# Attention turns of a two-layer encoder: minima and exponentials first, copies of turned probabilities last

## What is computed

```python
for l in range(DEPTH):                                   # 2 layers
    h = rms_norm(x, ln_g[l])
    proj = einsum('bsd,de->bse', h, w_in[l])             # q, k, v and gate columns of mixers A, B, C
    ya = window_sink_attention(...)                      # A: 12 heads, window of +-128 keys, sink, bias
    yb = global_axial_attention(...)                     # B: 12 heads, all keys of the sequence
    yc = dilated_mixture_attention(...)                  # C: 3 groups x 8 heads, merged by their denominators
    mix = concat(ya * silu(ga), yb * silu(gb), yc * silu(gc))
    x = x + einsum('bse,ed->bsd', mix, w_out[l])
```

## Time and profile before

| what | value |
|---|---|
| median of 3 runs | 2811.5 us (2803.23 to 2812.4) |
| time of the profiled execution | 2800.2 us |
| its span, first to last instruction | 2798.1 us |
| TensorE (PE) busy | 2763.8 us, 99% of the span |
| VectorE (DVE) busy | 1630.2 us, 58% |
| ScalarE (ACT) busy | 1226.2 us, 44% |
| GpSimd (POOL) busy | 932.6 us, 33% |
| DMA | 444.25 MB, mean 159 GB/s |
| granted TensorE clock | 1.000 of full speed |

### The profile page before, as it was taken

How to read it: one execution, slowest core, us unless ns; L and a number is a source line. 1 busy time by engine, 2 the same in 40 slices (tenths; PEclk the granted TensorE clock), 3 DMA queues, 4 the chain that set the end, 5 groups by cost and what they waited for, 6 DMA issues and landing times.

```text
span 2798.1 us, 44194 instructions
## 1 busy us (share of the span) xinstructions
PE 2763.8 (99%) x14913; PEld 2482.9 (89%) x14913; DVE 1630.2 (58%) x3973; ACT 1226.2 (44%) x3017; POOL 932.6 (33%) x860
## 2 busy tenths in 40 slices
PE   8999999999999999999999999999999999999999
PEld 7888899989999999988888888999899999998887
DVE  3446644434776677667743465444357766776776
ACT  4322222226665566544542222222266654664443
POOL 0333433310574377500003334333106733774000
PEclk9999999999999999999999999999999999999999
DMA  5366666569544432464624565666694444325645
GB/s 181 111 186 187 188 185 186 171 180 248 133 128 113 133 102 82 148 238 128 200 86 140 175 196 169 199 175 190 177 250 124 109 127 129 100 69 195 208 123 180
DMA packets 420602, 444.25 MB, mean 159 GB/s; under 512 B 62519, under 2 KB 314583, under 8 KB 420380
## 3 DMA queue, kind: packets, MB, share of 16 engines
q1 hardware_dynamic: 420380, 441.44, 53.4%
HBM read 315.54 MB, written 125.80 MB: 158 GB/s over the span
## 4 chain that ended last, share of the span: by engine, by line
PE 89%; DVE 3%; issue 2%; ACT 2%; POOL 2%; DMA 1%; SPq 0%; DVEq 0%; ACTq 0%; POOLq 0%
PE bank L1444 14%; PE bank L1442 14%; PE bank L1443 14%; PE bank L1498 5%; PE bank L1500 5%; PE bank L1499 5%; PE bank L1475 5%; PE bank L1477 5%; PE bank L1476 5%; PE bank L1541 4%; PE bank L1568 2%; PE bank L1527 2%; PE bank L1528 2%; PE bank L1583 2%; PE bank L1584 2%
## 5 line engine op out<-in xcount | busy, mean ns | idle before, releaser
L1916 DVE TENSOR_TENSOR w_lo<-w_raw,w_hi 128x512 fp32r<-128x512 f32 x640 | 458.3, 717 | 455.1 <-ACT w_hi L1652 451.0
L1652 ACT CAST w_hi<-w_raw 128x512 fp32r<-128x512 f32 x640 | 395.6, 619 | 686.7 <-PE bank L1444 417.5
L1442 PE MATMUL bank<-w_hi,act_hi 128*128 128x512 f32 x1728 | 688.9, 399 | 0.0
L1444 PE MATMUL bank<-w_hi,act_lo 128*128 128x512 f32 x1728 | 678.8, 393 | 0.0
L1443 PE MATMUL bank<-w_lo,act_hi 128*128 128x512 f32 x1728 | 677.3, 392 | 0.0
L2324 POOL TENSOR_SCALAR prob<-prob,denom 128x256 f32<-128x256 f32 (+2 forms) x288 | 345.9, 1205 | 270.0 <-DVE denom L2047 269.3
L1444 PEld LDWEIGHTS bank<-w_hi,act_lo 128*128 128x128 f32 x1728 | 372.4, 216 | 53.9
L1442 PEld LDWEIGHTS bank<-w_hi,act_hi 128*128 128x128 f32 x1728 | 373.2, 216 | 50.1
L1443 PEld LDWEIGHTS bank<-w_lo,act_hi 128*128 128x128 f32 x1728 | 373.1, 216 | 48.7
L1498 PE MATMUL bank<-act_hi,w_hi 128*128 128x384 f32 x1024 | 346.7, 339 | 0.0
L1500 PE MATMUL bank<-act_hi,w_lo 128*128 128x384 f32 x1024 | 344.9, 337 | 0.0
(11 more groups left out here) (121 smaller groups left out, 4636.6 us busy)
## 6 DMA issues: line engine op xcount, KB each, us to landing
w_raw<-w_in SPq DMA_DIRECT2D x144, 512.0 KB, 4.5
w_sums<-sum_out SPq DMA_DIRECT2D x32, 1280.0 KB, 6.7
w_raw<-w_sums SPq DMA_DIRECT2D x80, 512.0 KB, 4.1
sum_in<-w_out SPq DMA_DIRECT2D x64, 512.0 KB, 5.7
heads_t<-turned SPq DMA_DIRECT2D x240, 128.0 KB, 2.4
q_t<-heads_t SPq DMA_DIRECT2D x192, 128.0 KB, 2.1
k_t<-keys_t SPq DMA_DIRECT2D x48, 384.0 KB, 5.8
w_raw<-w_out SPq DMA_DIRECT2D x32, 512.0 KB, 3.7
```

What stands on the lines that cost most here:

```text
L1442: pe.matmul(acc[t][:], hi, w_hi[:, n % W_RING, :], start=(k == 0), stop=False)
L1444: last = pe.matmul(acc[t][:], lo, w_hi[:, n % W_RING, :], start=False, stop=(k == KC - 1))
L1652: nc.scalar.copy(w_hi[:, n % W_RING, :], w_raw[:, load % W_RAW, j, :]).then_inc(w_hi_done, 1)
L1916: nc.vector.tensor_tensor(w_lo[:, n % W_RING, :], w_raw[:, load % W_RAW, j, :], w_hi[:, n % W_RING, :].bitcast(F32), ALU.subtract).then_in ...
```

## The change

The order inside a turn of the attention is another on VectorE and on ScalarE; no instruction is added or removed, and TensorE, GpSimd and SyncE keep theirs. On VectorE `invert` and `find_minima` stand first, then `take_part`, the splits of the weights, the splits of the values, the merge, `add_folded` and `scale_gate`, and `pt_copy` last (ahead only of `a_lo_part`, in two turns). On ScalarE `keep`, `fold_pair` and the splits stand first, then `exp_step`, and `pt_copy` behind it. The splits of turn 0 are written ahead of the loop, where they stood first anyway.

```diff
--- before.py
+++ after.py
@@ -1853,19 +1853,22 @@
                             head_hi(l, s, t)
 
                 heads_in_dram(act, l)
+                for c in SPLIT_AT[0]:
+                    split_hi(l, CHUNKS_IN + c)
                 for i in range(N_LOOP):
-                    for c in SPLIT_AT.get(i, ()):
-                        split_hi(l, CHUNKS_IN + c)
+                    if ends_merge(i - KEEP_LAG):
+                        keep(l, STEPS[i - KEEP_LAG]["item"])
+                    if ends_pair(i - FOLD_LAG):
+                        fold_pair(l, i - FOLD_LAG)
+                    if i > 0:
+                        for c in SPLIT_AT.get(i, ()):
+                            split_hi(l, CHUNKS_IN + c)
                     if i in VALUES_AT:
                         values_hi(l, VALUES_AT[i])
-                    if ends_pair(i - FOLD_LAG):
-                        fold_pair(l, i - FOLD_LAG)
-                    if ends_merge(i - KEEP_LAG):
-                        keep(l, STEPS[i - KEEP_LAG]["item"])
+                    if i < N_STEPS:
+                        exp_step(l, i)
                     if 0 <= i - T_LAG < N_STEPS:
                         pt_copy(l, i - T_LAG)
-                    if i < N_STEPS:
-                        exp_step(l, i)
                     for mc, _ in merge_turns(i, EXP_TURN):
                         merge_exp(l, mc)
                     for n, h in TANH_AT.get(i, ()):
@@ -2221,19 +2224,20 @@
                             head_lo(l, s, t)
 
                 heads_in_dram(dve, l)
+                for c in SPLIT_AT[0]:
+                    split_lo(l, CHUNKS_IN + c)
                 for i in range(N_LOOP):
-                    for c in SPLIT_AT.get(i, ()):
-                        split_lo(l, CHUNKS_IN + c)
-                    if ends_quad(i - MIX_LAG):
-                        take_part(l, STEPS[i - MIX_LAG]["item"])
-                    if i in VALUES_AT:
-                        values_lo(l, VALUES_AT[i])
                     if 0 <= i - NORM_LAG < N_STEPS and features_first(STEPS[i - NORM_LAG]):
                         invert(l, i - NORM_LAG)
                     if i < N_STEPS:
                         find_minima(l, i)
-                    if 0 <= i - T_LAG < N_STEPS:
-                        pt_copy(l, i - T_LAG)
+                    if ends_quad(i - MIX_LAG):
+                        take_part(l, STEPS[i - MIX_LAG]["item"])
+                    if i > 0:
+                        for c in SPLIT_AT.get(i, ()):
+                            split_lo(l, CHUNKS_IN + c)
+                    if i in VALUES_AT:
+                        values_lo(l, VALUES_AT[i])
                     for mc, _ in merge_turns(i, MIN_TURN):
                         merge_minima(l, mc)
                     for mc, _ in merge_turns(i, WEIGHT_TURN):
@@ -2246,6 +2250,8 @@
                         add_folded(l, i - FOLD_LAG)
                     for n, h in GATE_DRAIN_AT.get(i, ()):
                         scale_gate(l, n, h)
+                    if 0 <= i - T_LAG < N_STEPS:
+                        pt_copy(l, i - T_LAG)
                     if i in EARLY_SPLIT:
                         a_lo_part(l, EARLY_SPLIT[i])
```

## The result

The changed kernel took 2817.3 us in the median of 17 runs (2808.67 to 2825.85), the kernel before 2802.1 us (2799.73 to 2812.4). The ratio is 1.0047 with a 95% interval of 1.0037 to 1.0056, about +13 us. In the profiled execution the span went from 2798.1 to 2815.7 us.

What follows compares the result with a forecast made beforehand. TensorE, busy 99% of the span, was taken as the bound. Q's loss of 11.2 us less gains of 7 (A and C) and 3 (B) gave +1.2 us, put on the 2811.5 us median as 2812.5 us; range 2799 to 2828.

Steps and rivals of the forecast that it cites:

- the likeliest case: Whole kernel: time within 0.3% of before, chance 0.48, with the forecast at 2812.5 us.
- Q, 11.2 us in both layers: Section Q (turns 0 to 23): ScalarE's later copies delay TensorE's value products, 5.6 us lost a layer.
- turn 5: Section Q: the copy behind step 4's exponentials ends later, so the value product starts 1.5 us later.
- turn 17: Section Q: turn 16's minimum waits 2.92 us for a store, so the value product starts 2.2 us later.
- turn 11: Section Q: turn 10's minimum waits 2.81 us for a store, so the value product starts 1.7 us later.
- the sum made of them: Section Q: the three delays add up, with 0.2 us for other even turns; 5.6 us a layer, bounds 2.2 and 8.
- A and C, 7 us gained: Sections A and C (turns 24 to 143): waits for minimum, `keep` and copy shrink, 3.5 us gained a layer.
- Nothing is added here: Sections A and C: the new order adds no cost, as VectorE's other work runs during ScalarE's exponential and high part.
- B, 3 us gained: Section B (turns 144 to 214): half of TensorE's 3.0 us of waits for exponentials goes, 1.5 us a layer.
- cost nothing in it: Section B: splits, `add_folded` and gate scaling fit VectorE's 2.0 us between minimum and low part, adding nothing to the chain.
- The chain in B as the bound: Rival, section B: the closed chain takes 0.1 us more a turn; +11 us, 2823 us, chance 0.25.
- GpSimd holds the split: Rival, section B: weight splits wait for GpSimd's normalisation to end, 0.9 us later; +15 us, 2827 us, chance 0.05.

Runs made afterwards that it cites:

- firstq: Changed kernel, but with ScalarE's copy of the turned probabilities ahead of its exponentials in turns 1 to 23, as before; 2806.1 us, ratio 1.0005.
- dve_only: Kernel before with VectorE's new order alone, in turns 1 and later, ScalarE keeping its old order; 2798.8 us, ratio 0.9983.
- swap_a: Kernel before with VectorE's new order from turn 24 on and ScalarE's new order in turns 24 to 95 alone; 2792.6 us, ratio 0.9968.
- slack: Changed kernel with two more reciprocals on VectorE ahead of the one in each turn of section B; 2830.1 us, ratio 1.0103.
- late4: Kernel before with ScalarE's copy of the turned probabilities behind the exponentials in turn 4 of each layer; 2811.9 us, ratio 1.0038.
- act_only: Kernel before with ScalarE's new order alone, in turns 1 and later, VectorE keeping its old order; 2986.1 us, ratio 1.0652.
- late16: Kernel before with ScalarE's copy of the turned probabilities behind the exponentials in turn 16 of each layer; 2814.1 us, ratio 1.0038.

## Why the prediction was right and where it was wrong

The time lay in the range (2799 to 2828), but the likeliest case was a change within 0.3% at 2812.5 us, and it came out slower by 0.47%. Part of the distance is the base: the forecast stood on a median of 2811.5 us, and the larger set of runs has 2802.1. On that base it would read +1 us; measured are about +13. So the base, 9 us too high, moved the forecast towards the measured time, and that it came within 5 us of it is in part luck.

- **Q, 11.2 us in both layers.** The mechanism held in each place. Turn 5 was to start its product 1.5 us late, and waited 1.50 in layer 1; turn 17 2.2, and waited 2.13 in both; turn 11 1.7, and waited 1.56 in layer 0. In the two other places TensorE was at half clock and didn't wait. The step that failed is the sum made of them: it took TensorE's clock as constant, and a stall as worth its own length. Q lost 23.9 us, 17.1 of them to the clock (3.4 of these behind a wait that isn't the change's), and the waits for copies came to 7.3 us instead of 11.2. It also put no price on VectorE's order in Q, where `part_out` is taken behind a waiting minimum; firstq and dve_only give that order 10 to 13 us in both layers together, clock included.
- **A and C, 7 us gained.** Measured 1.2 us. C gave 0.9 us a layer; the waits for a minimum and for `keep` went as said. The step that failed is "Nothing is added here": ScalarE's new order, its high part behind the exponential, does cost in A, 3.3 us a layer by swap_a, which uses up VectorE's gain of 2.9.
- **B, 3 us gained.** Measured 6.7 us. The chain was read rightly (2.67 us wide), its slack wrongly: none instead of 0.05 us a turn. The step that failed there is that splits, `add_folded` and a gate's scaling "cost nothing in it": the 2.0 us between minimum and low part are those of a turn of four tiles; where the low part is of two tiles the place is shorter, and a split, `add_folded` and the scaling don't fit into it (slack, 1095.29). Yet all the waits for exponentials went, not half. The term was mis-sized, 3.3 us a layer for 1.5.
- **The rivals.** The chain in B as the bound was nearest to happening (slack: 0.13 us more a turn costs 14 us) and did not cost. *GpSimd holds the split* did not happen either, but the row that it was judged by was not the whole story: in the earlier trace rows the split overlaps only the last 0.3 us of the normalisation. GpSimd, VectorE, then GpSimd again, in B of the changed kernel:

```profile
1123.13 1.57 POOL L2330 TENSOR_SCALAR prob<-prob,denom 128x512 f32<-128x512 f32 x1 [0.78 <-DVE denom L2050]
...
1123.54 0.82 DVE L1919 TENSOR_TENSOR w_lo<-w_raw,w_hi 128x512 fp32r<-128x512 f32 x1
...
1050.51 3.92 POOL L2330 TENSOR_SCALAR prob<-prob,denom 128x512 f32<-128x512 f32 x2
```

A split that starts 0.4 us into a normalisation takes 0.82 us instead of 0.69, and still ends 0.34 us before the normalisation does. The Trainium skill ("SBUF — State Buffer", section "SBUF: two separate sides") has the one blocked for the whole length of the other; by that rule the split could not have done anything before 1124.70. The trace disagrees for this pair; it shows a toll of 0.13 us. But the two aren't free of each other. Where the split starts first (1051.93), the normalisation that begins 0.12 us later takes 2.38 us instead of 1.57 (the second of the two in the last row), and beside GpSimd's product of two tensors a split takes 1.03 us (1080.60; 1.11 at 1038.86 in the kernel before), so the rival was judged for one pair and one order of start alone.

Had the runs' full-clock times been forecast (2803.0 at full clock, good to 2 us, against 2800.0 for the kernel before), +1.2 us would have been off by 2 us, partly by errors that cancel. What was missing is what the clock does with a stall in Q.

## What to carry to other kernels

Price a stall of TensorE by what its clock does afterwards, not by its length: in Q single waits of 0.9 to 2.2 us were followed by up to 10 us of lost clock, and with TensorE 99% busy that was lost time (in late4 15.4 us of clock, and Q 14.6 us longer). Take the price from rows of the same section, as in A and B most waits of that length were followed by none. Moving an instruction behind another that waits for a second engine closes a loop between two in-order engines; add up the loop once with the filler work inside it and once beside it, as the two orders (act_only and the changed kernel) differed by about 170 us here, and look whether the filler fits beside it in the shortest turn too. When a change reorders two engines, try each engine alone and each section alone: the kept half (one engine, three of four sections) was 0.65% faster where the whole was 0.47% slower.

## What the runs showed that was not expected

- The spread between a kernel's runs goes mostly with the clock: over the 17 runs of the changed kernel each 0.001 of mean clock is worth 2.3 us.
- ScalarE's order without VectorE's costs 6.5%, with the frequent instructions of VectorE and ScalarE as long as before (their medians within 0.03 us).
- The clock fell to half behind single waits of TensorE, for 3.4 to 20.5 us, but a wait's length alone doesn't decide it. In Q a wait of 0.94 us (late4) was followed by a fall, one of 1.56 us (turn 11 of the changed kernel) was not. In B the kernel before waits 1.20 us in both layers with no fall, and of twenty waits of 1.2 to 2.4 us in A, C and B of act_only only three had one at their end or within 0.8 us behind it. These 187 us of act_only (us, busy us and matmuls, granted clock, share of the DMA engines, GB/s) hold 24.0 us of waits for exponentials, the longest 2.4 us, at full clock:

```profile
1063.00:1250.00 187.00, 160.57 (x996) 1.00 0.23 67
```

What decides whether the clock falls, and for how long, stays open; late4 and late16 show that in Q a later copy is enough.
